# The feed-forward of a hybrid encoder step as seven half-size block products, with weight operands prepared in a stage of their own

## The reference, cut to what matters

```python
def conv_ffn(h, conv_state, w_gate_up, conv_w, conv_b, w_down):
    t = h.shape[1]
    gate, up = jnp.split(jnp.einsum("bsd,df->bsf", h, w_gate_up), 2, axis=-1)
    ext = jnp.concatenate([conv_state.astype(gate.dtype), gate], axis=1)
    conv = conv_b
    for i in range(CONV_W):                       # CONV_W = 3
        conv = conv + conv_w[i] * ext[:, i:i + t]
    y = jax.nn.silu(conv) * up
    return jnp.einsum("bsf,fd->bsd", y, w_down), ext[:, -(CONV_W - 1):]
```

## Time and profile before

| what | us |
|---|---|
| time of the timed runs, median of 2 | 2734.86 (2733.43 to 2736.3) |
| time of the profiled execution | 2734.05 |
| its span, first to last instruction | 2732.3 |
| mean granted TensorE clock | 0.977 of full speed |
| busy: TensorE, VectorE, ScalarE, GpSimd | 2608.4, 1376.9, 887.6, 189.9 |
| HBM read and written | 216.35 MB and 55.69 MB |

### The profile page before, as it was taken

The page is one execution under the profiler, slowest core; times in us unless marked ns, Lnnn a source line. Parts: engine busy times, 40 slices in busy tenths (PEclk is TensorE's granted clock), DMA queues, the critical chain, the costliest instruction groups (busy, mean ns, idle before and its releaser), DMA issues.

```text
span 2732.3 us, 45154 instructions
## 1 busy us (share of the span) xinstructions
PE 2608.4 (95%) x16553; PEld 2508.0 (92%) x16553; DVE 1376.9 (50%) x2973; ACT 887.6 (32%) x1696; POOL 189.9 (7%) x125
## 2 busy tenths in 40 slices
PE   5999999589999979969999999999999999999998
PEld 3888888489999979859999999999999999999998
DVE  5444444466767635565534552554355346625651
ACT  4233232476777633222212221222122222212220
POOL 0000000332322200000000002000000210000000
PEclk8999999799999989979999999999999999999999
DMA  7332321544434265562221223322122342221221
GB/s 210 91 95 82 92 83 59 122 113 94 94 78 101 53 222 181 199 236 67 72 74 61 69 87 120 127 69 79 60 69 68 106 145 67 78 69 62 69 87 64
DMA packets 192182, 271.61 MB, mean 99 GB/s; under 512 B 19138, under 2 KB 137890, under 8 KB 191970
## 3 DMA queue, kind: packets, MB, share of 16 engines
q1 hardware_dynamic: 184738, 246.13, 29.9%
q0 software_dynamic: 4848, 23.12, 2.4%
q10 hardware_dynamic: 2512, 1.26, 0.2%
HBM read 216.35 MB, written 55.69 MB: 100 GB/s over the span
## 4 chain that ended last, share of the span: by engine, by line
PE 55%; DMA 0%; DVE 0%; SPq 0%; POOL 0%; issue 0%; ACT 0%; POOLq 0%
PE ffn_z L81 55%; DMA ffn_acc<-h2T_scratch 0%; DVE ffn_h_lo L1644 0%; SPq L1484 0%; ACT ffn_h_hi L1590 0%; POOL yT L1535 0%; DVE ffn_acc L1701 0%; POOL gate_prompt L1541 0%; POOL gate_sample L1540 0%; SPq L1486 0%; POOLq L1539 0%; POOLq L1534 0%
## 5 line engine op out<-in xcount | busy, mean ns | idle before, releaser
L81 PE MATMUL ffn_z<-ffn_h_hi,ffn_w_hi 128*128 128x352 f32 x2112 | 680.8, 322 | 22.1 <-DVE ffn_w_lo L1639 22.0
L81 PE MATMUL ffn_z<-ffn_h_lo,ffn_w_hi 128*128 128x352 f32 x2112 | 680.2, 322 | 0.0
L81 PE MATMUL ffn_z<-ffn_h_hi,ffn_w_lo 128*128 128x352 f32 x2112 | 680.1, 322 | 0.0
L1581 ACT ACTIVATE ffn_w_hi<-ffn_w_raw 128x1024 fp32r<-128x1024 f32 (+1 forms) x180 | 205.6, 1142 | 716.8 <-PE ffn_z L81 715.8
L81 PEld LDWEIGHTS ffn_z<-ffn_h_hi,ffn_w_hi 128*128 128x128 f32 x2112 | 397.2, 188 | 24.2 <-DVE ffn_w_lo L1639 23.0
L81 PEld LDWEIGHTS ffn_z<-ffn_h_lo,ffn_w_hi 128*128 128x128 f32 x2112 | 397.5, 188 | 0.0
L81 PEld LDWEIGHTS ffn_z<-ffn_h_hi,ffn_w_lo 128*128 128x128 f32 x2112 | 397.5, 188 | 0.0
L81 PE MATMUL ffn_z<-ffn_y_lo,ffn_w_hi 128*128 128x352 f32 x1056 | 340.0, 322 | 0.0
L81 PE MATMUL ffn_z<-ffn_y_hi,ffn_w_hi 128*128 128x352 f32 x1056 | 339.7, 322 | 0.0
L81 PE MATMUL ffn_z<-ffn_y_hi,ffn_w_lo 128*128 128x352 f32 x1056 | 339.5, 321 | 0.0
L244 PE MATMUL project_z<-project_w_hi,project_h_hi 128*128 128x512 f32 (+3 forms) x680 | 256.7, 377 | 17.1 <-DVE project_w_lo L411 17.1
(11 more groups left out here) (149 smaller groups left out, 3793.4 us busy)
## 6 DMA issues: line engine op xcount, KB each, us to landing
ffn_w_raw<-w_gu SPq DMA_DIRECT2D x132, 512.0 KB, 3.6
ffn_w_raw<-w_dn SPq DMA_DIRECT2D x48, 704.0 KB, 4.0
combine_w_raw<-w_o SPq DMA_DIRECT2D x24, 512.0 KB, 5.1
combine_o_raw<-oT_scratch SPq DMA_DIRECT2D x12, 704.0 KB, 6.3
combine_x<-xT SPq DMA_DIRECT2D x12, 704.0 KB, 7.3
x1T_scratch<-combine_x SPq DMA_DIRECT2D x12, 704.0 KB, 7.5
ffn_acc<-x1T_scratch POOLq DMA_DIRECT2D x3, 2816.0 KB, 11.2
yT<-ffn_acc POOLq DMA_DIRECT2D x24, 352.0 KB
```

Source lines behind the costliest of these rows:

```text
L81: last = nc.tensor.matmul(out, w_parts[w](k), act_parts[a](k), start=(k == 0 and (w, a) == PASSES[0]), stop=(k == n_k - 1 and (w, a) == PA ...
L1581: nc.scalar.activation(w_hi[s][:, 0:n_k, :], w_raw[s][:, 0:n_k, :], ACT.Copy).then_inc(w_hi_ok[s], 1)
```

## The change

Both feed-forward products are written as 2 by 2 blocks: the operands' k-tiles are cut in halves, the outputs are a pair of tiles (gate and up, or two output tiles), and the tokens of a block are cut into the two halves of 352. Such a block product is made of seven products of half the k-length instead of eight (Winograd's form of Strassen's method). It needs sums of the operands:

- On the activation side the operands are A11, A12, A22 and the sums S1 to S4. They are made for every `unit` (one k-tile of each half): 4 sums (`sums_of_unit`), 7 casts on ScalarE and 7 subtractions on VectorE (`split_unit`).
- On the weight side a new stage, `prepare`, between `combine` and `ffn`, makes all seven operands of each block (three from sums on VectorE with one intermediate, `T1`, kept as an operand), splits them into high and low parts and writes both to memory (`w7_gu`, `w7_dn`). It works in 68 pieces with two buffers: SyncE loads four parts, VectorE makes the sums of piece n + 1 before it subtracts for piece n, ScalarE casts, GpSimd stores. `ffn` then reads the parts of each product straight into one of ten slots and splits no weights.
- The seven products of a group accumulate in pairs in PSUM banks, with readings in between: a bank is read after product 1, after 6 and after 7 while later products add on. Product 4 and 3 of a group come between the first ones of the next group. Product q of a group is one entry (g, q) of `products`, and all engines follow this list, without loops.
- The feed-forward width is done in parts of 2, 4, 4, 4, 4, 4 tiles; the down products of a part are put behind the second tile of the next part, those of the last part at the end of the block. The units for the next block's `h` are made during these last ones.
- SyncE issues only weight loads in `ffn`; the first loads of `h` go through ScalarE's queue; GpSimd no longer computes there.

The core of the diff:

```diff
+PART_SIZES = (2, 4, 4, 4, 4, 4)
+WINO_SLOTS = 10
+OPERANDS = ("A11", "A12", "A22", "S1", "S2", "S3", "S4")
+SLOT_OF = {1: 0, 7: 1, 3: 2, 2: 3, 5: 4, 6: 5, 4: 6}
+ACT_OF = {1: "A11", 2: "A12", 3: "S4", 4: "A22", 5: "S1", 6: "S2", 7: "S3"}
...
+    for b in range(N_BLOCKS):
+        for p, size in enumerate(PART_SIZES):
+            for i in range(size):
+                if i == 2 and p:
+                    for d in range(KD // 2):
+                        group("dn", b, p - 1, d)
+                group("gu", b, p, i)
+        for d in range(KD // 2):
+            group("dn", b, len(PART_SIZES) - 1, d)
+    for g, it in enumerate(groups):
+        late = g and not groups[g - 1]["flush"]
+        products.append((g, 1))
+        if late:
+            products.append((g - 1, 4))
+        products.append((g, 6))
+        if late:
+            products.append((g - 1, 3))
+        products += [(g, 7), (g, 2), (g, 5)]
+        if it["flush"] or g == len(groups) - 1:
+            products += [(g, 4), (g, 3)]
+    return groups, products
...
+            for c, (g, q) in enumerate(products):
+                it = groups[g]
+                if c >= R:
+                    sp.wait_ge(prod_ok, c - R + 1)
+                src = w7_gu[it["f"], SLOT_OF[q]] if it["kind"] == "gu" else w7_dn[it["p"]][it["i"], SLOT_OF[q]]
+                sp.dma_start(w[c % R][:, :, 0:it["nk"], :].bitcast(F32), src).then_inc(w_ld[c % R], 16)
...
+                u = h_unit(b, k)
+                pool.wait_ge(op_lo_ok, len(OPERANDS) * u)
+                for half in range(2):
+                    pool.dma_start(y_raw[:, half, :], h2T[k + HK * half, :, b * BLOCK:(b + 1) * BLOCK]).then_inc(h_ld, 16)
...
+            def store(g):
+                it = groups[g]
+                pool.wait_ge(c11_ok, g + 1)
+                pool.wait_ge(c21_dn_ok, it["n"] + 1)
+                pool.wait_ge(add12_ok, it["n"] + 1)
+                pool.wait_ge(add22_ok, it["n"] + 1)
+                rows = slice(2 * it["i"], 2 * it["i"] + 2)
+                pool.dma_start(yT[rows, :, it["b"] * BLOCK:(it["b"] + 1) * BLOCK].rearrange("k p n -> p k n"), acc[:, rows, :])\
+                    .then_inc(y_st, 16)
...
+                for g in finals:
+                    it = groups[g]
+                    if it["b"] == b and b < LAST:
+                        load_h(b + 1, it["i"])
+                    if it["b"] == b:
+                        store(g)
...
+            def read_back(g, q):
+                it = groups[g]
+                if q == 1 and g > 1:
+                    old = groups[g - 2]
+                    pe.wait_ge(c21_gu_ok if old["kind"] == "gu" else c21_dn_ok, old["n"] + 1)
+                elif q == 6:
+                    pe.wait_ge(x_gu_rd if it["kind"] == "gu" else x_dn_rd, it["n"] + 1)
+                elif q == 7:
+                    pe.wait_ge(sum2_ok, g + 1)
+                elif q == 4:
+                    pe.wait_ge(sum3_ok, g + 1)
+                elif q == 2 and g > 1:
+                    pe.wait_ge(c11_ok, g - 1)
+                elif q == 5 and g > 1:
+                    pe.wait_ge(c12_ok, g - 1)
+                elif q == 3:
+                    pe.wait_ge(c22_ok, g + 1)
...
+            for c, (g, q) in enumerate(products):
+                it, name = groups[g], ACT_OF[q]
+                hi, lo = (h_hi, h_lo) if it["kind"] == "gu" else (y_hi, y_lo)
+                bank = {1: x_ps, 6: x_ps, 7: x_ps, 4: x_ps, 2: y_ps, 5: z_ps, 3: z_ps}[q][g % 2]
+                first, last = q in (1, 2, 5), q in (4, 2, 3)
+                fresh = (it["kind"] == "gu" and it["p"] == 0 and it["i"] == 0) or (it["kind"] == "dn" and it["i"] == 0)
+                pe.wait_ge(w_ld[c % R], 16 * (c // R + 1))
+                read_back(g, q)
+                for k in range(it["nk"]):
+                    if fresh:
+                        pe.wait_ge(op_lo_ok, unit_done(unit_at(g, k), name))
+                    for wp, a in PASSES:
+                        mm = nc.tensor.matmul(
+                            bank[:, 0:SUB], w[c % R][:, wp, k, :], (hi, lo)[a][name][:, k, :],
+                            start=first and k == 0 and (wp, a) == PASSES[0],
+                            stop=last and k == it["nk"] - 1 and (wp, a) == PASSES[-1], skip_group_check=True)
+                mm.then_inc(prod_ok, 1)
...
+            for k in range(HK):
+                for half in range(2):
+                    nc.scalar.dma_start(acc[:, k + HK * half, :], h2T[k + HK * half, :, 0:BLOCK]).then_inc(h0_ld[k], 16)
...
+                if it["flush"] and q == 3:
+                    split_unit(unit_of(g))
+                if q in SPREAD:
+                    u = unit_after(g)
+                    if u is not None:
+                        split_unit(u, SPREAD[q])
+                if q == 2 and it["kind"] == "dn" and it["p"] == len(PART_SIZES) - 1 and it["b"] < LAST:
+                    split_unit(h_unit(it["b"] + 1, it["i"]))
...
+            def sums_of_unit(u):
+                loaded(dve, u)
+                a11, a12, a21, a22 = (source(u, n) for n in ("A11", "A12", "A21", "A22"))
+                dve.wait_ge(op_hi_ok, len(OPERANDS) * u)
+                dve.wait_ge(op_lo_ok, len(OPERANDS) * u)
+                nc.vector.tensor_tensor(s_raw["S1"][:], a21, a22, ALU.add).then_inc(s1_ok, 1)
+                nc.vector.tensor_tensor(s_raw["S3"][:], a11, a21, ALU.subtract).then_inc(s3_ok, 1)
+                dve.wait_ge(s1_ok, u + 1)
+                nc.vector.tensor_tensor(s_raw["S2"][:], s_raw["S1"][:], a11, ALU.subtract).then_inc(s2_ok, 1)
+                dve.wait_ge(s2_ok, u + 1)
+                nc.vector.tensor_tensor(s_raw["S4"][:], a12, s_raw["S2"][:], ALU.subtract).then_inc(s4_ok, 1)
+            def split_unit(u, names=OPERANDS):
+                for name in names:
+                    dve.wait_ge(op_hi_ok, unit_done(u, name))
+                    nc.vector.tensor_tensor(target(u, name, False, True), source(u, name),
+                                            target(u, name, True, False).bitcast(F32), ALU.subtract).then_inc(op_lo_ok, 1)
...
+                it = groups[g]
+                dve.wait_ge(acc_ld, 16 * (it["b"] + 1))
+                part = acc[:, 2 * it["i"], T1]
+                nc.vector.tensor_tensor(part, part, x_ps[g % 2][:, 0:SUB], ALU.add).then_inc(x_dn_rd, 1)
+            def evict(g, q, c):
+                it = groups[g]
+                gu = it["kind"] == "gu"
+                if q == 1 and not gu:
+                    dve.wait_ge(prod_ok, c + 1)
+                    add_x(g)
...
+                elif q == 5:
+                    dve.wait_ge(prod_ok, c + 1)
+                    dve.wait_ge(sum3_ok, g + 1)
+                    up = sum3[g % 2]
+                    nc.vector.tensor_tensor(up[:], up[:], z_ps[g % 2][:, 0:SUB], ALU.add).then_inc(c22_ok, 1)
...
+                if q == 5 and it["kind"] == "dn":
+                    add22(g)
+                if q == 3 and it["kind"] == "dn":
+                    add12(g)
+                if q == 5 and it["kind"] == "gu":
+                    first_half(g)
+                if q == 6 and waiting:
+                    second_half(g - 1)
+                if q == 7 and waiting:
+                    times(g - 1, 0)
+                    times(g - 1, 1)
+                if q == 7 and unit_after(g) is not None:
+                    sums_of_unit(unit_after(g))
+                if it["flush"] and q == 4:
+                    second_half(g)
+                if it["flush"] and q == 3:
+                    times(g, 0)
+                    times(g, 1)
+                    sums_of_unit(unit_of(g))
+                    split_unit(unit_of(g))
+                if q in SPREAD and unit_after(g) is not None:
+                    split_unit(unit_after(g), SPREAD[q])
+                if q == 2 and it["kind"] == "dn" and it["p"] == len(PART_SIZES) - 1 and it["b"] < LAST:
+                    sums_of_unit(h_unit(it["b"] + 1, it["i"]))
+                    split_unit(h_unit(it["b"] + 1, it["i"]))
...
+def prepare(nc, w_gu, w_dn, w7_gu, w7_dn):
+    HK = KD // 2
+    starts = [sum(PART_SIZES[:p]) for p in range(len(PART_SIZES))]
+    pieces = []
+    for f in range(D_FF // P):
+        for k in range(0, HK, 2):
+            src = [w_gu[f, s, :, k + at:k + at + 2, :] for s, at in ((0, 0), (1, 0), (1, HK), (0, HK))]
+            pieces.append((2, src, [w7_gu[f, :, :, part, k:k + 2, :] for part in range(2)]))
+    for p, size in enumerate(PART_SIZES):
+        half = size // 2
+        for i in range(KD // 2):
+            src = [w_dn[2 * i + s, :, starts[p] + at:starts[p] + at + half, :]
+                   for s, at in ((0, 0), (1, 0), (1, half), (0, half))]
+            pieces.append((half, src, [w7_dn[p][i, :, :, part, :, :] for part in range(2)]))
+    N = len(pieces)
+    with ExitStack() as ctx:
+        m = Memory(nc, ctx, "prepare")
+        ops = [m.sbuf(f"ops{i}", [P, 7, 2, P]) for i in range(2)]
```

(140 more changed lines are left out.)

429 lines of the change are left out of this document (193 added, 236 removed).

## The result

The changed kernel takes 3377.92 us (median of 2 runs, 3376.21 to 3379.63) against 2734.86: 1.2357 times as long [1.2337, 1.2377], 643 us more. The forecast was 3510. The profiled execution took 3376.21 us, its span 3373.9.

The account below looks back on a forecast made before the run. TensorE's matmuls were taken to bound the feed-forward. 2734 plus 820 for the preparing stage, less 44 (189 of matmuls saved, 145 of new waits), gave 3510 us; forecast 3400 to 3620, stated range 3210 to 3650.

Parts of the forecast that it names:

- rival (a): Preparing stage: loads not held up (even byte shares or small store packets), landing at 5.1 us; total 3317; chance 0.24.
- 8.1 us: Preparing stage, full piece: four loads land after 1.1 to first packet, 6.7 beside the stores, 0.3 to land.
- the step: Preparing stage: one semaphore step releases loads and two stores; 1 KB load packets each wait for a 4 KB one.
- Rival (b): Preparing stage runs at the DMAs' own rate, 6.7 us a piece: stage 451, total 3141; chance 0.10.
- (c): More DMA-bound: slow stores in the preparing stage, or weight stream delaying TensorE 50 to 100 us; 3620 to 3720; chance 0.14.
- (d): Not slower: preparing hidden beside earlier stages if no barrier held it; then 2690; chance 0.02.
- start: Feed-forward start: four units of sums and subtractions before the first product can end; +14 us, and 3 for the clock.
- ends of the gate parts: End of each block's gate part: 9.1 us of work with 0.95 of matmuls meanwhile, 25 us over three.
- last down groups, blocks 0 and 1: Feed-forward: adds, next block's operands and a load behind a store hold TensorE; 52 us, plus 10 for half-busy groups.
- other down groups, half-size groups: Feed-forward: VectorE's bank read between products 1 and 6, 13 us over 52 groups; 18 us for 12 half-size groups.
- 13 us for 6.7 of matmuls: Each last down group of blocks 0 and 1: 7 adds, 11 operand operations, a load landing in 3.7 us.
- the 3, 9 and 10 us: Feed-forward clock allowances: 3 at the start, 9 for three or more stops, 10 for the half-busy last groups.

Follow-up runs that it names:

- the first two experiments: Changed kernel with only 4 of 68 pieces prepared: 2754.64 us; kernel before with the preparing stage added, its output unread: 3395.05 us.

## Why the prediction was right, point by point

**The sign and the mechanism held.** It named TensorE as the bound, the barrier-closed stage as the price, and the chain of loads, sums and subtraction as what sets the piece. All three are shown: by the split of the 643 us, by the row of VectorE's waits, and by four buffers taking 236 us off. The size was less good than that. The time is 132 us under the forecast: some 157 too much for the stage, less 23 too much given back by the feed-forward. It is below the 3400 to 3620 that the forecast had for itself, and nearer to rival (a), 3317, though neither condition of (a) came true: the store packets were large and the turns not even in bytes. It is inside the stated 3210 to 3650 because that range had been drawn down over (a).

**The stage was 157 us too dear: 663 for 820.** Per piece 9.7 us for 12.2, which over 64 pieces is 160:

| term | forecast | measured |
|---|---|---|
| loads land | 8.1 | 6.08 |
| four sums with gaps | 1.95 | 1.60 |
| subtraction | 2.0 | 2.02 |
| neighbours | 0.1 | 0 |

The mis-sized term is "8.1 us" for the loads. The store packets did hold 4 runs (4096 B), which had been a guess that no row showed. That loads and stores go packet by packet in turn, which the term takes as given, no run shows as a rule; what was measured is 223 to 212 packets in 1508:1511, and a wait of 6.08 us. Two sizes were off. At the 350 GB/s taken, or 21.9 for each of 16 engines, a 4096 B packet is 187 ns; it took 159. And the step let loads and stores start together, while SP's first packet comes 0.95 us after its issue and GpSimd's 1.6 to 2.0 us (here 1.8, at 1507.94) after an issue that is itself 0.28 later. So in 1506.5:1508 the loads had sent 218 data packets and 21 of 4 B when the stores had sent 5. The other 294 of 512 are 18.4 for each DMA engine, each in turn with a store packet: 18.4 x (159 + 46) ns = 3.8 us. From the issue at 1505.89 to 1508 are 2.1; with 0.3 to land (in the kernel without stores VectorE starts 0.33 after the end of the last packet, at 1506.25) it is 6.2 us, and 6.08 was measured. That is an estimate by even turns, and it comes out closer than it deserves: in 1511:1511.5 the loads sent 123 packets and the stores 36.

**But the step's reason is only half upheld.** The 83 to 79 packets of the two queues in 1219:1221 of the kernel before had been taken for turns packet by packet. In 1508:1511 of the kernel after the counts agree (223 to 212); in 1511:1511.5 (36 to 123) and with ScalarE's stores (670 to 284) they do not. The consequence that I drew, that small store packets would free the loads, fell in two experiments: with 1 KB packets on both sides the wait grew from 6.08 to 8.10 us, with the sides swapped to between 8.68 and 8.88. What holds the loads back there is shown only as far as the packets go: in one, stores alone for 1 us between two loads, and then over two store packets for each of the loads; in the other, the loads' first packet 3.6 us after their issue. What the cause is stays open.

**Rival (b)** failed for the reason given (a piece is not at the DMAs' rate while two buffers chain it), and its price was right: 451 forecast, 427 with four buffers. **(c)** did not come: the weight stream ran at 270 GB/s with TensorE busy 376.50 of 380.00 us, and it took a cut to four slots to uncover it. Its time was added up wrongly, though: a stream that alone holds TensorE up by 50 to 100 us gives 3560 to 3610, not 3620 to 3720. **(d)** is excluded for this kernel by the first two experiments: the whole stage adds to the time. What it names as its one mechanism, the stage beside the ones before, no run tries. Over their 1199 us, 155.7 MB would be 130 GB/s more, where the DMA digits are 1 to 7; whether that would hide the stage stays open.

**The feed-forward gave back 21 us, not 44.** The stage less its matmuls is 1512.1 - 1325 = 187 us after and 1533.2 - 1514 = 19 before, so the new waits are 168 for 145. In the stream a matmul still takes 380 / 2350 = 0.162 us at most, so the 189 were saved. A stretch less 0.1593 us for each of its matmuls gives the waits by place (2802:2902 counts 11.6 for its gate end, as does 2302:2334):

| place | forecast | from the stretches | measured |
|---|---|---|---|
| start | 14 + 3 | 40 - 64 x 0.1593 = 30, before 10 | 20 |
| ends of the gate parts | 25 + 9 | 3322:3342: 20 - 53 x 0.1593 = 11.6; x 3 | 35 |
| last down groups, blocks 0 and 1 | 52 + 10 | 14.5 + 43.3 + 56.4 - 2 x 11.6 | 91 |
| other down groups, half-size groups | 13 + 18 | 1942:1962 4.4, 2442:2482 5.6, 2902:2982 7.5 | 18 |

The end, forecast at 1, and what is spread over the stream are the other 4. Clock included, start and gate ends were sized well. The mis-sized term is "13 us for 6.7 of matmuls" in the last down groups, 29 us too little: a group takes 21 (2347.62 to 2368.84), since the load of `h`, issued behind a 704 KB store of `yT` with the weight stream in the other queue, lands after 7.3 to 9.7 us and not 3.7 (3.8 in the first group, which has no store ahead), and VectorE stands for it. Own tiles and earlier loads take 51 us away, so that wait is shown to be on the path. What the low clock there (0.67 of full speed in 2334:2402, TensorE busy 33.35 us of 68.00) adds by itself, no run parts from the waits. So no run shows the 3, 9 and 10 us that the forecast has for the clock; what was granted is 0.55 in 1862:1902, 0.67 in 2334:2402, 0.78 in 2802:2902 and 0.66 in 3322:3342. The smaller places were 13 us too dear: outside the half-size part I find hardly a gap at product 6.
